# The stores of the expert results move from GpSimd's queue to ScalarE's, and the x transposes move behind the first down chunk

## The reference, cut to what matters

```
for e in range(16):                                  # D = 1024, F = 512
    hid = silu(xt @ W_gate_e[e]) * (xt @ W_up_e[e])
    y = y + combine[:, e:e + 1] * (hid @ W_down_e[e])
```

## Time and profile before

| | |
|---|---|
| time, median of 3 runs | 1492.91 us (1490.84 to 1498.19) |
| the profiled execution: its own time | 1478.94 us |
| its span | 1477.3 us, mean granted TensorE clock 0.899 |
| TensorE matmuls, weight loads | 1162.9 us (79%), 966.4 us (65%) |
| VectorE, ScalarE, GpSimd | 840.9 us (57%), 642.4 us (43%), 214.3 us (15%) |
| the experts' stage | from about 898 to 1418 us |

### The profile page before, as it was taken

One profiled execution on the slowest core, in us unless ns is written; L12 is line 12 of the kernel. 1 busy time (PEld: TensorE's weight loads), 2 busy tenths in 40 slices (PEclk: granted clock), 3 DMA queues, 4 the chain that ended last, 5 costly groups with the idle time before them and its releaser, 6 DMA issues. The chain is left out here.

```text
span 1477.3 us, 24630 instructions
## 1 busy us (share of the span) xinstructions
PE 1162.9 (79%) x8079; PEld 966.4 (65%) x8080; DVE 840.9 (57%) x1669; ACT 642.4 (43%) x1154; POOL 214.3 (15%) x307
## 2 busy tenths in 40 slices
PE   4199888988798879988489953997899989898910
PEld 3197767867596759776368843776777767677810
DVE  2715872388426861588456676486654455456339
ACT  4424543355344542454412215475544445346324
POOL 0201220022101210122000111101100011001132
PEclk9699998999899989999699976999999999999965
DMA  9322312222123212131442417799856695766156
GB/s 334 112 76 57 86 41 57 79 65 69 49 65 90 69 33 70 50 110 50 144 130 86 136 61 243 272 316 333 293 192 215 201 319 190 243 227 227 57 185 213
DMA packets 202730, 215.80 MB, mean 146 GB/s; under 512 B 15640, under 2 KB 167824, under 8 KB 202368
## 3 DMA queue, kind: packets, MB, share of 16 engines
q1 hardware_dynamic: 180400, 174.89, 37.6%
q0 software_dynamic: 10064, 34.42, 6.4%
q10 hardware_dynamic: 12192, 5.41, 1.4%
HBM read 187.89 MB, written 26.79 MB: 145 GB/s over the span
## 5 line engine op out<-in xcount | busy, mean ns | idle before, releaser
L710 PE MATMUL mixers_ps_proj<-early_h_hi,mixers_w_hi 128*128 128x352 f32 x384 | 129.2, 336 | 36.5 <-POOL mixers_a_hg L486 27.6
L1758 PE MATMUL experts_ps_g<-experts_w_hi,experts_x_hi 128*128 128x512 f32 x384 | 152.5, 397 | 2.2 <-DVE experts_x_lo L1679 2.2
L1760 PE MATMUL experts_ps_g<-experts_w_hi,experts_x_lo 128*128 128x512 f32 x384 | 150.3, 391 | 0.0
L1759 PE MATMUL experts_ps_g<-experts_w_lo,experts_x_hi 128*128 128x512 f32 x384 | 150.0, 391 | 0.0
L1673 DVE TENSOR_TENSOR experts_w_lo<-all_raw,experts_w_hi 128x2048 fp32r<-128x2048 f32 x48 | 109.7, 2288 | 65.6 <-ACT experts_w_hi L1621 57.8
L736 PE MATMUL mixers_ps_proj<-mixers_w_hi,early_h_hi 128*128 128x512 f32 (+1 forms) x288 | 127.7, 444 | 9.9 <-DVE mixers_w_lo L864 9.9
L499 POOL TENSOR_TENSOR mixers_k_lv<-mixers_decay,mixers_hk 128x1024 f32<-128x1024 f32 (+2 forms) x40 | 79.1, 1982 | 342.6 <-ACT mixers_decay L575 342.6
L711 PE MATMUL mixers_ps_proj<-early_h_lo,mixers_w_hi 128*128 128x352 f32 x384 | 127.1, 331 | 0.0
L712 PE MATMUL mixers_ps_proj<-early_h_hi,mixers_w_lo 128*128 128x352 f32 x384 | 127.0, 331 | 0.0
L737 PE MATMUL mixers_ps_proj<-mixers_w_lo,early_h_hi 128*128 128x512 f32 (+1 forms) x288 | 120.7, 419 | 0.0
L738 PE MATMUL mixers_ps_proj<-mixers_w_hi,early_h_lo 128*128 128x512 f32 (+1 forms) x288 | 120.5, 418 | 0.0
(11 more groups left out here) (269 smaller groups left out, 2567.7 us busy)
## 6 DMA issues: line engine op xcount, KB each, us to landing
experts_raw_more<-in_W_down_e_dram SPq DMA_DIRECT2D x128, 256.0 KB
all_raw<-in_W_gate_e_dram SPq DMA_DIRECT2D x96, 256.0 KB, 6.3
all_raw<-in_W_up_e_dram SPq DMA_DIRECT2D x96, 256.0 KB, 6.5
all_raw<-in_W_in_dram SPq DMA_DIRECT2D x32, 512.0 KB, 5.4
all_raw<-in_W_ada_dram SPq DMA_DIRECT2D x32, 512.0 KB, 5.6
y_scratch<-experts_y POOLq DMA_DIRECT2D x24, 512.0 KB
condition_w_ada_in<-in_W_ada_dram SPq DMA_DIRECT2D x4, 2048.0 KB, 11.2
experts_raw_more<-in_W_gate_e_dram SPq DMA_DIRECT2D x32, 256.0 KB
```

The lines of the kernel that those rows point to most:

```text
L710: pe.matmul(out, whi, xhi, start=(k == 0), stop=False)
L1758: pe.matmul(out, x_hi[:, k, :], w_hi[:, c, at], start=(k == 0), stop=False)
L1759: pe.matmul(out, x_hi[:, k, :], w_lo[:, c, at], start=False, stop=False)
L1760: ins = pe.matmul(out, x_lo[:, k, :], w_hi[:, c, at], start=False, stop=(k == KD - 1))
```

## The change

GpSimd keeps the gathers alone. The store of `y`, the reading of its first row from `s.plan`, and the first small store that opens the count `y_stored` go to ScalarE. ScalarE issues the store of a tile behind the split of pair 5. In ScalarE's order `pair(3)` and `h_high(1)` come ahead of `x_high(t)`. In VectorE's order `product(0)` comes ahead of `pair(0)` and `h_low(0)` ahead of `pair(1)`. In TensorE's order `turn_x(t)` moves from ahead of the first down chunk to behind it.

```diff
             gather(slice(0, 1), 1)
-            pool.dma_start(s.y_scr[SLOTS:SLOTS + P, 0:P], ident).then_inc(y_stored, 16)
 
             def tile(x, t, j, last, last_expert):
-                start = pool.value_load(s.plan[0:1, bass.ds(x, 1)], min_val=0, max_val=SLOTS)
-                row = pool.snap(start + j * P, min_val=0, max_val=SLOTS)
-
...
                 pool.wait_ge(xt_done, pool.snap(t + 1))
                 carry(pool, idle)
                 gather(column, pool.snap(t + 2))
-                pool.wait_ge(y_stored, pool.snap(t * 16 + 16))
-                pool.wait_ge(y_done, pool.snap(t + (1 + PRIMED)))
-                carry(pool, idle)
-                pool.dma_start(s.y_scr[bass.ds(row, P), :], y[:, :]).then_inc(y_stored, 16)
...
                 pair(2)
                 silu(1)
+                pair(3)
+                h_high(1)
                 x_high(t)
-                h_high(1)
-                pair(3)
                 pair(4)
+                start = act.value_load(s.plan[0:1, bass.ds(x, 1)], min_val=0, max_val=SLOTS)
+                row = act.snap(start + j * P, min_val=0, max_val=SLOTS)
                 act.wait_ge(used, act.snap(t * CH + CH))
                 act.wait_ge(y_stored, act.snap(t * 16 + 16))
                 act.activation(y[:, :], ps_y.rearrange("p m n -> p (m n)"), ACT.Copy).then_inc(y_done, 1)
                 pair(5)
+                act.wait_ge(y_done, act.snap(t + (1 + PRIMED)))
+                carry(act, idle)
+                act.dma_start(s.y_scr[bass.ds(row, P), :], y[:, :]).then_inc(y_stored, 16)
 
             act.preload_act_table_set("silu_and_others")
+            act.dma_start(s.y_scr[SLOTS:SLOTS + P, 0:P], ident).then_inc(y_stored, 16)
...
+                product(0)
                 pair(0)
-                product(0)
+                h_low(0)
                 pair(1)
-                h_low(0)
                 product(1)
...
-                turn_x(t)
                 pe.wait_ge(y_done, pe.snap(t + PRIMED))
                 for f in range(KF):
                     if f == 1:
+                        turn_x(t)
                         turn_h(1)
```

## The result

The changed kernel takes 1413.29 us (median of 4 runs, 1410.87 to 1417.11) against 1491.88 us for before beside it (4 runs, 1484.89 to 1498.19): ratio 0.9477, 95% interval 0.9429 to 0.9525. A repetition on another occasion, with more runs (6 and 17), gave 1411.73 against 1482.1 us: 0.9513, interval 0.9476 to 0.9551. The direction was right.

A forecast was written before the change was run, and what follows sets the result against it. TensorE bounds the experts' stage, stalled by late gathers behind GpSimd's store. -69.5 + 1.5 + 5 - 2.5 = -65.5 us gives 1413.4 from the profiled 1478.94, or 1427 on the median's footing; range 1415 to 1453.

The forecast's parts named there:

- 69.5 us: Experts' stage, time beyond unhindered tiles: 41.3 waits for x, 6.4 waits for `hid`, 21.8 lower clock; the most tiles can give.
- +1.5 for the waits for `hid`: One-tile experts that follow another: ScalarE's store and loop code delay `pair(0)`; +1.5 us, bounds nothing to 6.4.
- Rival A: ScalarE's queue becomes the head of the tile at expert changes: 24 us in place of 1.5, time 1450; chance 0.12.
- +5 for the DMA load: Tiles 3 to 6, four one-tile experts: 3.0 us of lateness each at 354 GB/s, less 4 in hand; bounds 0 and +14.
- the reserve: One-tile experts: 4 us between the last down loads' landing and ScalarE's `pair(5)` wanting them, absorbing DMA lateness.
- Rival B: DMA engines bind wherever an expert has one tile: seven tiles gain nothing, 42 of 69.5 us stay, time 1465; chance 0.06.
- -2.5 at the end of the stage: Last store of y, issued by ScalarE instead of GpSimd: 2.5 us saved, between 0.7 and 3.4.
- The start at nothing: Stage start: the small store ahead of ScalarE's first split takes 0.4 us, ahead of the late first gather; costs nothing.
- The moved transposes and ScalarE's order at nothing: TensorE's `turn_x` behind the first down chunk, ScalarE's `pair(3)` ahead of `x_high`: no term of their own in the sum.
- The margin of 0.35 us for the low part of h: Split tiles: `h_low(1)` ends at 15.05, third down chunk wants it at 15.4; a miss was priced with nothing.

## Why the prediction was right or wrong

**The mechanism: right.** The gather hung on the order of GpSimd's queue, and the 14 waits for x and the lower clock went with the stores. Shown by the profile after and by the kernel in which only the stores move (all waits for x gone). What the prediction did not see is that, in tiles with an expert of their own, some 1.2 to 1.9 us of the gather's lateness in before stood beside VectorE's `pair(0)`. It cost the forecast nothing: at its new place the gather's issue takes 0.94 to 1.01 us in every tile of the changed kernel's three executions.

**"69.5 us": right for the one execution, 2.6 too small for the mean.** Four profiles give 72.1.

**+1.5 for the waits for `hid`: measured 0.5 in the mean, and in another place.** I bounded ScalarE's loop code by 2.8 us because it had no idle time before. Behind the store it takes 1.9 to 3.4 us, so that bound was wrong. In tile 13 of the first execution `pair(0)` is at S + 4.18 (4.7 reckoned) and silu at 6.0 (6.6), and nothing waits. In three of the 21 tiles with an expert of their own (tile 3 twice, tile 13 once) `pair(0)` is at S + 4.75 to 5.32, and the tile is 0.2 to 0.8 us longer. No wait for `hid` ahead of `turn_h(0)` came; in tile 13 TensorE waits for the low part of h. Rival A falls as priced (24 us), but its mechanism is there, and a second store on the same queue brings it out at 4.6 us.

**+5 for the DMA load: measured 3.8 in the mean, by two errors that work against each other.** The rate was 369 GB/s, not 354, so a tile lags by 2.15 us (19.90 less 17.75), not 3.0. And the reserve was 1.5, 3.2 and 3.1 us in the three executions (three lags less the excess of tiles 4 to 6, 4.95, 3.25 and 3.31), not 4: I took the last down load as the one that is wanted first, but ScalarE waits for earlier pairs. In tile 6 of the changed kernel, which starts at 1020.44, this is `pair(1)` in ScalarE's timeline, 2.13 us late:

```profile
1028.75 1.92 ACT L1612 ACTIVATE experts_w_hi<-all_raw 128x2048 fp32r<-128x2048 f32 x1 [2.13 <-DMA all_raw<-in_W_up_e_dram]
```

Rival B falls: tiles 13, 16 and 21 show no wait for weights, even with 0.52 MB more per tile.

**-2.5 at the end of the stage: 2.9. The start at nothing: 1.0.**

**The moved transposes and ScalarE's order at nothing: right,** shown by the kernel that puts them back. The margin of 0.35 us for the low part of h held in every tile but those where ScalarE waited for weights, and tile 13 of the third execution.

**The step that failed** is the last of the sum: "Its time lies 14 us under the median of the runs, 1492.91, which I can't resolve by stage; on the median's footing the forecast is 1427". I carried the whole 14 us over to the changed kernel. It does not have them: its profiled execution took 1410.87, and its ten runs average 1412.7. On the mean of the 45 later runs of before, 1484.4, the same sum gives 1418.9, inside the range: 8.5 of the 14 us are the amount by which the median of three runs lay above that mean. The other 5.4 are a profiled execution that was quicker than the mean. Some 2.6 of them lay in the tiles' excess, which the change removes and does not carry; the rest lay outside it and is not explained. From 1418.9 to the measured 1412.7 remain 6.1 us, and these are the terms above: 2.6 for the excess, 2.5 for the tiles of the changed kernel (4.0 in place of 1.5 + 5), 0.4 for the end and 1.0 for the start, 6.5 in all. The range failed with that step. Its low end took 5 us for the scatter of runs, though two footings 14 us apart lay open, 1413.4 and 1427; a low end that held the first could not have been above 1413.

**What stays open:** why the first runs of before were slower than the 45 later ones (four of them, 1484.89 to 1498.19, one of which is above all 45). Chance alone is not likely, since they average 1491.7 and the 45 scatter with a standard deviation of 4.3 us around 1484.4. Another chip would do; on which one they ran is not known, and no profile of those three runs exists. That the waits for x vary explains a few us of the scatter, not 8.5. Open too is why ScalarE's loop code takes 1.9 us in one tile and 3.4 in another.

## What to carry to other kernels

Where two DMAs that wait for different things share one engine's queue, look for the time at which each could go out by its data: here the gather was ready 12 us before its turn. A stall that hangs on a queue's order can swallow a gain ahead of it (in tile 13 of before the 1 us won at `hid` was lost at x), so remove it first and judge the rest again. A queue that takes over a DMA can become the next head of the tile: here one more store on ScalarE's queue lengthened four tiles by 4.6 us in all. And make the sum and the range against both footings, the profiled execution and the runs: a difference between them may be scatter, and may lie in the very waits that the change removes.

## What the runs showed of the hardware that I had not expected

**GpSimd waits for VectorE's split.** In before this held the issue of the gather back in 26 of 28 tiles (0.97 us alone, 2.2 to 2.8 beside `pair(0)`, ending 0.85 us after it), as told above. In the changed kernel it meets the copy of the index. That copy of one column of 128 numbers took 0.18 us in some tiles and up to 2.30 in others. The timeline of the changed kernel in tile 5 shows why:

```profile
1014.44 2.28 DVE L1670 TENSOR_TENSOR experts_w_lo<-all_raw,experts_w_hi 128x2048 fp32r<-128x2048 f32 x1
1014.47 2.30 POOL L1582 COPY experts_index<-experts_lists 128x1 int32 x1 [15.87 <-PE experts_ps_x L1728]
```

The copy starts 0.03 us after VectorE's subtraction and ends 0.05 us after it, at 1016.77. The same is seen in tile 6 (1034.51 to 1036.70, where the split ends at 1036.65) and in tile 3 (0.62 us, ending 0.05 us after the split). The Trainium skill (SBUF — State Buffer, "SBUF: two separate sides") says that the two engines lock a shared pair of ports for a whole instruction, among others when VectorE has two inputs in SBUF and GpSimd reads SBUF; the trace agrees. In the changed kernel it costs nothing, since the gather has some 7 us of margin.

**A wait does not always bring the lower clock.** In before 14 waits, most of about 3 us, cost 21.8 us of slower matmuls, but unevenly: eleven tiles lost 1.8 to 2.1 us beyond their waits, the other three 0.2 to 0.4. Behind a wait of 2.85 us the eight transposes at 1116.49 took 1.09 us, and the granted clock was 1.00 from 1116.5 to 1122; behind one of 3.07 us those at 1030.04 took 1.97, and it was 0.73 from 1030 to 1036. With the orders alone, twelve of the 14 tiles lost 0.2 us beyond their waits of 0.6 to 3.15 us, and two lost 1.8, behind waits of 3.18 and 3.07. So a shorter wait saved more than its own length: 18.5 us of waits and 16.0 of lower clock.
